# A two-layer hybrid trunk in fp32: 64x64 tiles for the recurrence's diagonal blocks, half steps and pair products, and another order at the start

## The reference

```python
def trunk_layer(xc, xl, c, c_ctx, cos, sin, p, ctx_out):
    mod_l = split(silu(c) @ ada_w + ada_b, 6)        # modulation of the latent tokens
    mod_c = split(silu(c_ctx) @ ada_w + ada_b, 6)    # and of the context tokens
    hl, hc = modulate(xl, norm1_g, ...), modulate(xc, norm1_g, ...)
    (ab, ac, ax, rkv, wl, al, gl, q, k, v, gate) = split_cols(h @ w_in)      # both segments
    att_l = windowed_attention(...)                  # latent on latent window and context
    r, v, kk, decay, k_d, b_d, g = rwkv_inputs(rkv, wl, al, gl)
    s_ctx, y_rc = rwkv_scan(0, context inputs, emit=ctx_out)                 # 16 heads, 2 directions
    _, y_rl = rwkv_scan(s_ctx, latent inputs, emit=True)
    xl = xl + mod_l[2] * merge(conv_l, rwkv_l, att_l, gates) ; xl = xl + mod_l[5] * conv_ffn(...)
    if ctx_out: the same for xc                      # layer 1 only

def step(S, inp):                                    # rwkv_scan, per head and direction
    sa = S @ at ; S = S * wt + outer(sa, bt) + outer(vt, kt) ; y = S @ rt
```

## Time and profile before

| | |
|---|---|
| median of 3 runs | 2762.18 us (2760.99 to 2764.26) |
| the profiled execution's own time | 2767.3 us |
| its span | 2765.5 us |
| PE busy | 2694.9 us (97%), 26901 records |
| PEld busy | 1733.2 us (63%) |
| DVE busy | 1403.6 us (51%) |
| ACT busy | 734.9 us (27%) |
| POOL busy | 215.0 us (8%) |
| chain that ended last | PE 92%, ACT 4%, DVE 2%, issue 2% |
| mean granted clock | 0.994 |

### The profile page before, as it was taken

How to read it: one execution, slowest core, us unless ns; L and a number is a source line. 1 busy time by engine, 2 the same in 40 slices (tenths; PEclk the granted TensorE clock), 3 DMA queues, 4 the chain that set the end, 5 groups by cost and what they waited for, 6 DMA issues and landing times.

```text
span 2765.5 us, 61050 instructions
## 1 busy us (share of the span) xinstructions
PE 2694.9 (97%) x26901; PEld 1733.2 (63%) x26901; DVE 1403.6 (51%) x2723; ACT 734.9 (27%) x1502; POOL 215.0 (8%) x184
## 2 busy tenths in 40 slices
PE   7999999999999999999999999899999999999999
PEld 3455555556444446748888444566666677787887
DVE  2676666674322233337778112777777633314541
ACT  3234333442222221111111003333443322211110
POOL 1000000000000002214444000000000000000000
PEclk9999999999999999999999999999999999999999
DMA  7211111111334333345533224212221233356554
GB/s 262 57 50 43 50 43 51 50 40 43 116 90 120 85 115 95 102 126 156 156 108 106 69 76 142 59 51 59 59 58 51 52 113 107 107 145 188 153 149 120
DMA packets 500007, 264.52 MB, mean 96 GB/s; under 512 B 42864, under 2 KB 493888, under 8 KB 499232
## 3 DMA queue, kind: packets, MB, share of 16 engines
q1 hardware_dynamic: 498016, 251.58, 31.3%
q0 software_dynamic: 1728, 9.03, 0.9%
HBM read 255.33 MB, written 5.24 MB: 94 GB/s over the span
## 4 chain that ended last, share of the span: by engine, by line
PE 92%; ACT 4%; DVE 2%; issue 2%; POOL 0%; DMA 0%; POOLq 0%; ACTq 0%; DVEq 0%
PE psum L515 35%; PE psum L517 14%; PE psum L1179 12%; PE psum L1291 8%; PE psum L779 2%; PE psum L549 2%; PE psum L1012 1%; PE psum L888 1%; PE psum L1000 1%; PE psum L590 1%; PE psum L990 1%; PE psum L729 1%; PE psum L769 1%; PE psum L756 1%; PE psum L902 1%
## 5 line engine op out<-in xcount | busy, mean ns | idle before, releaser
L515 PE MATMUL psum<-hT,strips 128*128 128x256 f32 (+1 forms) x2252 | 710.4, 466 | 1.2 <-issue 1.2
L515 PEld LDWEIGHTS psum<-hT,strips 128*128 128x128 f32 x2252 | 420.9, 192 | 229.6 <-issue 192.1
L517 PE MATMUL psum<-hT,strips 128*64 128x512 f32 (+1 forms) x1896 | 393.5, 535 | 2.6 <-DVE arena L2364 1.4
L1291 PE MATMUL psum<-arena,strips 128*128 128x512 f32 (+1 forms) x704 | 227.6, 486 | 0.6 <-DVE arena L2803 0.6
L1291 PEld LDWEIGHTS psum<-arena,strips 128*128 128x128 f32 x704 | 133.7, 190 | 93.0 <-issue 83.2
L517 PEld LDWEIGHTS psum<-hT,strips 128*64 128x64 f32 x1896 | 116.4, 136 | 108.5 <-issue 85.0
L515 PE MATMUL psum<-arena,strips 128*128 128x256 f32 (+1 forms) x416 | 125.9, 461 | 0.9 <-DVE done L2652 0.9
L2803 DVE SCALAR_TENSOR_TENSOR arena<-psum,mod,arena 128x256 f32<-128x256 f32 x24 | 10.9, 480 | 193.7 <-PE psum L1291 193.7
L515 PEld LDWEIGHTS psum<-arena,strips 128*128 128x128 f32 x416 | 78.9, 190 | 45.0 <-issue 36.8
L2185 DVE TENSOR_SCALAR arena<-arena 128x512 f32<-128x512 f32 (+1 forms) x88 | 69.7, 792 | 70.5 <-ACT arena L2040 68.1
L1179 PE MATMUL psum<-arena,rwkv_branch 128*128 128x256 f32 x424 | 99.0, 379 | 0.0
(11 more groups left out here) (303 smaller groups left out, 4166.9 us busy)
## 6 DMA issues: line engine op xcount, KB each, us to landing
strips<-in_w_in_dram SPq DMA_DIRECT2D x152, 512.0 KB, 3.8
strips<-in_ada_w_dram SPq DMA_DIRECT2D x80, 512.0 KB, 4.9
strips<-in_ffn_up_dram SPq DMA_DIRECT2D x46, 512.0 KB, 3.8
strips<-in_ffn_down_dram SPq DMA_DIRECT2D x32, 512.0 KB, 3.8
conv_branch<-in_ffn_up_dram SPq DMA_DIRECT2D x28, 512.0 KB, 4.8
arena<-in_ada_w_dram SPq DMA_DIRECT2D x4, 2048.0 KB, 14.6
strips<-in_w_in_dram SPq DMA_DIRECT2D x32, 256.0 KB, 3.4
strips<-in_a_out_w_dram SPq DMA_DIRECT2D x16, 512.0 KB, 3.8
```

The costliest lines, as they stand in the source:

```text
L515: return pe.matmul(o, lhs, rhs, start=start, stop=stop, skip_group_check=True)
L517: ins = pe.matmul(o[64 * h:64 * h + 64], lhs[:, 64 * h:64 * h + 64], rhs, start=start, stop=stop, skip_group_check=True)
L1291: ins = mm(s.o[:, lo:T], strip[:, b, j, :], hid[:, k, lo:T], k == 0, k == FT - 1)
```

## The change

- `constants`: the masks `strict32` and `unit32` become 64 wide, with zeros where a column is of the other 32x32 block.
- `diagonal_blocks`: whole 64x64 products, 32 matmuls. The off-diagonal parts are computed and masked away. `LB` (128x1024) takes the masked result; it lies where `MV` lies. DVE sums its two halves into `LC` for the inversion (one more instruction, with a wait before and behind it).
- POOL adds the unit diagonal to `LB` instead of `LC`. `half_step` takes `LB` as stationary, 64x64, with `T16` moving, 32 matmuls on two tiles.
- `pair_products`: where `n` is 64 (context chunks of layer 2), the stationary 64x128 is split into two of 64x64, four matmuls a chunk for two.
- The diagonal blocks of unit `i + 1` come right behind `outputs_of_states`, ahead of the last hop's fill.
- `low_rank`: the third strip of layer 2 covers the latent tokens only, on PE and on ACT.
- The start: `ada_unit(0)` goes ahead of `spread_tokens` and `turn_params`, `ada_unit(1)` behind them, both picks follow in `low_rank`. SP loads the ada units 2 and 3 behind the first low-rank strip and ahead of the other two. DVE spreads the norm factors ahead of its last copy of `xT`, and scales three row tiles ahead of the modulation and five behind. ACT copies ada unit 0 ahead of the norm factors.

```diff
+    side = (p // 32 % 2)[:, None] == (np.arange(64) // 32)[None, :]
+    cols["strict64"] = side & (np.arange(64)[None, :] % 32 > u)
+    cols["unit64"] = side & (np.arange(64)[None, :] % 32 == u)
...
+        LB = MV.rearrange("p m d h t -> p (m d h t)").rearrange("p (s t) -> p s t", t=64)
...
+                pe.wait_ge(ev["c_ready"], 1)
+                ada_unit(0)
+                spread_tokens()
                 turn_params(0)
-                spread_tokens()
-                pe.wait_ge(ev["c_ready"], 1)
+                ada_unit(1)
...
+                steps = fresh_strips([(A, ("low0", l)), (A, ("low1", l)), (G, ("low2", l))],
+                                     (0, 0, 0 if l == 0 else SEG), 2 * l)
...
-                    for b in range(2):
-                        for c in range(NCH):
-                            p, m = c % 2, c // 2
-                            for d in range(2):
+                    for m in range(4):
+                        for d in range(2):
+                            for p in range(2):
+                                c, n = 2 * m + p, (4 * d + m) * CH
                                 for h in range(2):
-                                    o = PS[quad(2 * p + b), b0 + h, (4 * d + m) * 32:(4 * d + m + 1) * 32]
-                                    ins = one(o, BK[d][rows(h), c, p, 32 * b:32 * b + 32],
-                                             ar[d][rows(h), c, 0, 32 * b:32 * b + 32])
+                                    ins = one(PS[rows(p), b0 + h, n:n + CH], BK[d][rows(h), c, p, :], ar[d][rows(h), c, 0, :])
...
-                        for h in range(2):
+                        for e in range(2 if n == CH else 0):
+                            for h in range(2):
+                                ins = one(PS[rows(e), b0 + h, (c % 4) * n:(c % 4 + 1) * n], BK[d][rows(h), c, e, :],
+                                         ar[d][rows(h), c, 0, :])
+                        for h in range(2 if n == P else 0):
...
-                        for q in range(4):
-                            ins = one(PS[quad(q), b0, t * 32:(t + 1) * 32], LC[quad(q), t, :], T16[quad(q), t, :])
+                        for p in range(2):
+                            ins = one(PS[rows(p), b0, t * 32:(t + 1) * 32], LB[rows(p), t, :], T16[rows(p), t, :])
...
                         if c == NCH - 1:
                             outputs_of_states(i)
+                            if ahead:
+                                diagonal_blocks(i + 1)
                         if c > 0:
                             fill(steps, hop)
...
-                    if ahead:
-                        diagonal_blocks(i + 1)
                     fill(steps, everything)
...
                 for c in (COL_W, COL_AL, COL_G):
                     load(wcols(wi, c))
+                    if l == 0 and c == COL_W:
+                        load_unit(512)
+                        load_unit(D + 512)
                 if l == 0:
-                    load_unit(512)
-                    load_unit(D + 512)
...
-                    pool.tensor_tensor(LC, LC, tab["unit32"].unsqueeze(1).broadcast_to([P, SLOTS, 32]), ALU.add)\
+                    pool.tensor_tensor(LB, LB, tab["unit64"].unsqueeze(1).broadcast_to([P, SLOTS, 64]), ALU.add)\
...
-                    tt(LC.rearrange("p (h s) t -> p h s t", h=2),
-                       PS[:, b0:b0 + 2, 0:256].rearrange("p h (s t) -> p h s t", t=32),
-                       tab["strict32"].unsqueeze(1).unsqueeze(1).broadcast_to([P, 2, 8, 32]), MUL).then_inc(s.free, 1)
+                    tt(LB, PS[:, b0:b0 + 2, :].rearrange("p h (s t) -> p (h s) t", t=64),
+                       tab["strict64"].unsqueeze(1).broadcast_to([P, SLOTS, 64]), MUL).then_inc(s.free, 1)
                     dve.wait_ge(*s.freed)
+                    t = did(tt(LC, LB[:, :, 0:32], LB[:, :, 32:64], ADD))
+                    dve.wait_ge(*t)
```

More of the change, by code:

```diff
@@ L94, in constants @@
     u, v = (p % 32)[:, None], np.arange(32)[None, :]
-    cols["strict32"] = v > u
-    cols["unit32"] = v == u
+    side = (p // 32 % 2)[:, None] == (np.arange(64) // 32)[None, :]
+    cols["strict64"] = side & (np.arange(64)[None, :] % 32 > u)
+    cols["unit64"] = side & (np.arange(64)[None, :] % 32 == u)
     cols["half32"] = (v == u) | ((u >= 16) & (v < 16))
@@ L533, in strip_steps, with fresh_strips @@
                     yield (T - first) // SEG
-            def fresh_strips(takes, first, n):
+            def fresh_strips(takes, firsts, n):
                 ss, bs, frees = [], [], []
@@ L545, in fresh_strips @@
                         for k in range(4 * half, 4 * half + 4):
-                            for e, (t0, t1) in enumerate(halves(n) if (j, k) == (0, 0) else ((first, T),)):
+                            for e, (t0, t1) in enumerate(halves(n) if (j, k) == (0, 0) else ((firsts[j], T),)):
                                 if j == 0:
@@ L673, in begin @@
                     ins.then_inc(s.full[0], 1)
+                pe.wait_ge(ev["c_ready"], 1)
+                ada_unit(0)
+                spread_tokens()
                 turn_params(0)
-                spread_tokens()
-                pe.wait_ge(ev["c_ready"], 1)
+                ada_unit(1)
             def low_rank(l):
-                steps = fresh_strips([(A, ("low0", l)), (A, ("low1", l)), (G, ("low2", l))], 0, 2 * l)
+                steps = fresh_strips([(A, ("low0", l)), (A, ("low1", l)), (G, ("low2", l))],
+                                     (0, 0, 0 if l == 0 else SEG), 2 * l)
                 def pick(u):
@@ L684, in low_rank @@
                 if l == 0:
-                    for u in range(2):
-                        ada_unit(u)
-                        pick(u)
+                    pick(0)
+                    pick(1)
                     next(steps)
@@ L1268, in ada_between @@
                         pick_turn(G, 1, 3, 2)
-                for _ in fresh_strips([(A, up(0, 0)), (A, up(0, 1))], lo, 2 * l + 1):
+                for _ in fresh_strips([(A, up(0, 0)), (A, up(0, 1))], (lo, lo), 2 * l + 1):
                     pass
@@ L1642, in begin @@
                 act.activation(token_rs, token_rs, ACT.Exp, scale=-0.5).then_inc(ev["token_ready"], 1)
+                ada_part((0, 0), part[:, 0, :])
                 s = await_slot("norm", 0)
@@ L1647, in begin @@
                 for half in range(2):
-                    for u in range(2 * half, 2 * half + 2):
+                    for u in range(max(2 * half, 1), 2 * half + 2):
                         if u > 1:
@@ L1660, in low_rank @@
                 s = await_slot("low2", l)
-                act.activation(low[:, 2, :], s.o, ACT.Tanh, scale=0.5).then_inc(s.free, 1)
+                lo = 0 if l == 0 else SEG
+                act.activation(low[:, 2, lo:T], s.o[:, lo:T], ACT.Tanh, scale=0.5).then_inc(s.free, 1)
                 act.wait_ge(*s.freed)
-                act.activation(low[:, 2, :], low[:, 2, :], ACT.Copy, bias=0.5, scale=0.5).then_inc(ev["low_ready"], 1)
+                act.activation(low[:, 2, lo:T], low[:, 2, lo:T], ACT.Copy, bias=0.5, scale=0.5).then_inc(ev["low_ready"], 1)
                 act.wait_ge(ev["low_ready"], l + 1)
@@ L2111, in square, with scaled @@
                         dve.wait_ge(*order.next())
-            def scaled(n, lo):
-                for k in range(KT):
+            def scaled(n, lo, k0=0, k1=KT):
+                for k in range(k0, k1):
                     for e, (t0, t1) in enumerate(halves(n) if k == 0 else ((lo, T),)):
@@ L2119, in scaled @@
                         tt(hT[:, k, t0:t1], xT[:, k, t0:t1], rs[:, t0:t1], MUL).then_inc(ev["xn_ready"], 1)
-                dve.wait_ge(ev["xn_ready"], h_count(n, KT - 1))
+                dve.wait_ge(ev["xn_ready"], h_count(n, k1 - 1))
             def gain(l, scale, g, k0, k1):
@@ L2165, in begin @@
                     dve.tensor_copy(xT[:, 2 * u:2 * u + 2, :], PS[:, BANK_P[s.b]:BANK_P[s.b] + 2, :]).then_inc(s.free, 1)
[L2166 to L2169, removed]
+                    if u == 2:
+                        dve.wait_ge(ev["token_ready"], 1)
+                        for j in range(4):
+                            ins = ts(rs_rows[:, j, :], ones[:, :], token_rs[:, j:j + 1], None, MUL)
+                        ins.then_inc(ev["rows_ready"], 1)
                 setup(0)
-                ts(sink[:, :, :], sink[:, :, :], -1.0, None, MUL)
-                scaled(0, 0)
+                scaled(0, 0, 0, 3)
                 for half in range(2):
@@ L2180, in begin @@
                     gain(0, KT, pp[:, 15, :], 4 * half, 4 * half + 4)
+                    if half == 0:
+                        scaled(0, 0, 3, KT)
+                        ts(sink[:, :, :], sink[:, :, :], -1.0, None, MUL)
             def conv(dst, src, g0, g1, g2, release=None, last=None):
```

## The result

| | before | after |
|---|---|---|
| median of the runs | 2761.59 us (4 runs) | 2785.91 us (4 runs, 2783.52 to 2787.77) |
| ratio | | 1.009, 95% interval 1.0078 to 1.0103 |
| the profiled execution's own time, its span | 2767.3, 2765.5 us | 2787.8, 2786.0 us |
| PE busy, records | 2694.9 us, 26901 | 2710.6 us, 25109 |
| DVE busy | 1403.6 us | 1441.6 us |

The change made the kernel 24.3 us slower by the medians, outside the range of 2744 to 2775, and 27.9 above the forecast 2758. The two traces differ by less: the span grew by 20.5 us, because the traced execution before stands some 5 us above its median and the one after 1.9. By stages (from one `diagonal_blocks` to the next, read off the timelines of PE): start -2.4; unit 0 +4.9; units 1 to 6 +11.1; unit 7 and all up to layer 2 +2.0; first unit of layer 2 -7.7; the next six +8.2; the rest +4.5.

The account below looks back on a forecast made before the run. PE was taken to bound the kernel, with issue halts and DVE's transposes delaying it in layer 2. Terms 22.0 - 20 - 3.4 - 2.5 = -3.9 gave 2763.4 us, 2758 on the median's footing; range 2744 to 2775.

Parts of the forecast that it names:

- part 5: PE's instruction fetch in the recurrence: 27 us of issue halts saved, 7 given back to low clock, net -20 us.
- the third rival: Low clock comes in every unit where PE now waits, nine times 1.7 instead of 7: +8, 2766 us; chance 0.09.
- the pool is 38: Time put down to PE's issue halts, mostly in layer 2's units: 38 us, of which 27 was taken as saved.
- Diagonal blocks: 32 products of 64 columns on four tiles take 0.9 us instead of 1.33, so 0.4 saved.
- Half step: With 64x64 stationary on two tiles it takes 1.8 us instead of 1.22: +0.6 on PE, 16 times.
- The pair-product row: Profile row of layer 2's pair product, about 0.13 us a round, read as stationary width setting the round.
- DVE's chain: DVE's steps up to the half step grow 2.5 us: wider eviction +0.53, added LC sum 0.72, select behind POOL +1.2.
- part 4: DVE's longer chain, less the blocks' earlier start, set against each unit's slack on PE; the recurrence sums to +22.0 us.
- The rest of the recurrence: Units of layers 1 and 2 without the instruction-fetch and low-clock terms: +22.0 us.
- Third strip -3.4 and start -2.5: Layer 2's third low-rank strip over fewer columns saves 3.4 us; the reordered start lets low-rank strips begin sooner, saving 2.5.
- DVE's longer waits let the fetch catch up: PE's longer waits for DVE give its code fetch time; one reason for taking 27 us of halts as saved.
- The halts stay: Rival: issue halts remain in layer 2 while DVE's longer chain is paid in full, 2785 us with all kept; chance 0.26.

Follow-up runs that it names:

- e1: Changed kernel with two dense steps moved ahead of the half step in units 0 to 6 of layer 1 and six units of layer 2: 2771.7 us.
- e3: Changed kernel with the half step in 64 products of 32x32 again, taken out of LB: 2760.8 us.
- e12: e6 with the pair products of layer 2 whole again (one 64x128 product): 2749.8 us.
- e6: Changed kernel with the 32x32 half step out of LC and POOL adding to LC, keeping the 64x64 diagonal blocks: 2737.7 us, ratio to before 0.9915.
- e7: Changed kernel with the pair products of layer 2 whole again (one 64x128 product instead of two of 64x64): 2802.4 us.
- e9: e6 with four dense steps moved ahead of the half step in unit 0 of layer 1: 2734.0 us, ratio to before 0.9903.
- e10: e6 with one dense step moved ahead of the half step in six units of layer 2: 2738.7 us.
- e2: Kernel before, with the eviction of the diagonal blocks done four times in a row on DVE: 2798.1 us.

## Why the prediction was wrong

The step that failed is the last of part 5: "waits of 2 to 4 us were followed by the low clock before; four times 3.4 us at half is +7". The clock fell in unit 0 and in twelve of the other fifteen units, for 3.4 or 6.8 us each, and half of it is lost (77.60 against 76.00). By the mean clock, (0.994 - 0.985) x 2786 = 25 us for 7: 18 of the 24.4 by which the sum missed the profiled execution (+20.5 for -3.9). It is a bound more than a measurement, since it takes PE to set the time in every low stretch. In the sixteen units alone the clock was low for 61.4 us against 20.5 before, 20.5 us at half; the other 5 lie outside them. I had the mechanism as the third rival and priced it at 1.7 in each of nine units, unit 0 and those of layer 2; it came in layer 1's other units too, behind a wait of 1.0 us, where e1 without the wait and e3 without the 64-wide half step had none, and in layer 2 it lasted up to 6.8 us instead of 3.4. Of the 27.9 us between 2758 and the median 2785.9 the last 3.5 are footing and rounding: I took 5.1 off for the profiled execution, and the one after stands only 1.9 above its median.

The other 6 us are in the size of "the pool is 38" (its terms add up to 37). It was made of the surplus of layer 2's units over the shortest one, and in that surplus lay also the low clock behind the halts (20 us of it at half, so 10). Issue waits went from 22.7 to 1.7 us in the whole kernel: -21, where I took -27.

Point by point:
- Diagonal blocks: 0.9 forecast, 1.1 measured (103.76 to 104.85, 182.99 to 184.12). Half step: 1.8 forecast, 1.88 to 1.99 at full clock. The pair-product row was the right guide: a round of 0.06 us costs about what 64 columns cost, not 32. Whether that is the stationary tile's width or the two tiles at work instead of four, no run varies by itself. (By the Trainium skill, "TensorE: Matmul & The Clock Gate", section "LDWEIGHTS (loading the stationary operand)", it would be 1.7, an estimate at about 0.83 ns a column; measured it is 0.2 to 0.3 more.)
- DVE's chain: 1.22, 0.69 and 2.74 where 1.22, 0.72 and 2.8 stood. The wait in layer 2 is 2.09, where "about 2.5" was named.
- Layer 1, units 1 to 6 without the low clock: 76.0, 1.0 above before, where 0.9 was forecast. Unit 7, for which part 4 took 0.5 off, waited 1.03 like the others: its slack in the kernel before was for the most part an issue wait of 1.16 us at 632.9, and that went. Unit 0: +4.9, 3.4 of them clock; 2.7 was forecast.
- The rest of the recurrence by difference: 20.5 + 2.4 + 3.4 + 21 - 25 = +22, as forecast (+22.0). By difference only, so with the error of the 25: no run times it alone.
- Third strip -3.4 and start -2.5: -3.3 (19.20 to 15.9 in e12, where no low clock lies in it) and -2.4. AL did not delay the second strip.
- "DVE's longer waits let the fetch catch up" was right and weighed too little: e1 takes most of the waits away and has 14.6 us of issue waits with the same instructions.
- "The halts stay", the rival that ends at 2785 too, is false: the time agrees, the trace does not.

What I did not ask is which part of the change brings what. e6 answers it: without the half step on 64x64 and the wider LB addition that only it needs, the change is worth 24 us. The addition costs 23 (e3 less e6), of which some 16 are its own 1.1 us in fifteen units; the half step costs 25 (after less e3), of which 12 are its own. The rest of both, 7 and 13, goes with the low clock (mean 0.997, 0.992 and 0.985) and, in the first, 2 us of issue waits.

**What stays open.** Why low stretches come in every second unit of layer 1, and why a few appear where nothing was changed. In the changed kernel the stretch at 1700 is low behind the same waits that left the clock up in the kernel before, as this row for each, the changed kernel first, shows:

```profile
1700.00:1707.00 7.00, 6.66 (x8) 2.45 (x9) 3.68 (x9) 6.99 (x13) 0.00 (x0) 0.51 1.03 314
```
```profile
1681.00:1690.00 9.00, 6.79 (x17) 2.82 (x18) 5.80 (x13) 8.97 (x17) 0.00 (x0) 1.00 1.04 381
```

The local wait alone does not decide it; the moment at which it falls may, as in e7, but no run sets that by itself. Nor was the fetch varied alone: that the split pairs lower the issue waits though they add instructions speaks for where a block of code ends, which was not tried by itself.

## What to carry to other kernels

A wait of one or two us in front of short, sparsely packed products can cost twice itself, by the low clock behind it (in e6 a wait of 1.0 us cost no more than itself): bound a longer chain by its wait plus half of the low stretch in every iteration, and fill the wait with dense work that is due anyway, as e1 did in layer 1 and e9 in unit 0. Fewer, wider products do not gain by their number alone (the half step with half the records took 2.0 us for 1.2), and what they need elsewhere (here twice the columns on POOL, behind which DVE stands) is part of their price. Before idle time is booked as a gain, see what else it pays for: in e10 it had paid for the fetch of PE's code.

## What the runs showed of the hardware

- The granted clock fell to 0.5 behind waits as short as 1.0 us, in four of seven units, when the half step of 2.0 us on two tiles followed. With the one of 1.2 us on four tiles it stayed up behind the same wait in seven of seven (e3), fell in one of seven behind 1.4 to 1.6 us (e2, layer 1) and in five of seven behind 1.9 and 2.1 us (e2 and e3, layer 2).
- PE's issue waits stand where its instruction count is 193 to 195 above a multiple of 256, in the same 126 cases. The count is that of the PE records before the one that waits: matmuls, loads and the sequencer's own (1036 in the kernel before; without these the place drifts); queue 8 moves a packet of 16.4 KB for 256 of them. In e6 five of eight units have a wait in `corner_below`, 1.2 us in the first and 0.2 to 0.4 in the others; in e1 a wait of 3.2 us comes in every second unit. More instructions can mean less waiting: e12 has 16 products a unit of layer 2 fewer than e6 (64 records with their loads) and 9.7 us of issue waits against 2.5.
- DVE's select of 256 columns took 1.62 or 2.74 us beside an addition of 512 or 1024 columns on POOL that started within 0.05 us of it and took 1.29 or 2.40. Where the select took 0.48, in unit 0 of nine of the kernels, the addition took 0.3 more, 1.58 or 2.70: one of the two always stood.
